# The experts' order in a mixture stage: two sparse experts behind each dense one

## The reference

```python
group_p = softmax(t @ w_group + b_group); g_w, g_idx = top_k(group_p, 1)
...
combine = g_w * one_hot(g_idx, N_GROUPS) * expert_w      # two experts of the token's group
for g in range(N_GROUPS):                                # 4 groups of 8 experts
    hg = silu(einsum('nd,edf->nef', t, w_gate[g])) * einsum('nd,edf->nef', t, w_up[g])
    y = y + einsum('nef,efd->nd', hg * combine[:, g, :, None], w_down[g])
```

## Time and profile before

| | us |
|---|---|
| median of 3 runs | 2664.12 |
| lowest and highest | 2663.37, 2664.22 |
| the profiled execution | 2666.28 |
| its span, first to last instruction | 2664.5 |

### The profile page before, as it was taken

The page is one execution under the profiler, slowest core; times in us unless marked ns, Lnnn a source line. Parts: engine busy times, 40 slices in busy tenths (PEclk is TensorE's granted clock), DMA queues, the critical chain, the costliest instruction groups (busy, mean ns, idle before and its releaser), DMA issues.

```text
span 2664.5 us, 45241 instructions
## 1 busy us (share of the span) xinstructions
PE 2621.3 (98%) x18380; PEld 2331.7 (88%) x18380; DVE 1802.6 (68%) x2201; ACT 1419.5 (53%) x1882; POOL 142.7 (5%) x229
## 2 busy tenths in 40 slices
PE   9999999999999999999989999999999999999999
PEld 8889989788898888879988888889988888889887
DVE  6667788766657666679757666666566676665765
ACT  6555567644555455458435455453355454455544
POOL 4000000100000000000210000000100000000000
PEclk9999999999999999999999999999999999999999
DMA  7187899655535555544305556556356555554553
GB/s 219 45 271 259 269 315 352 216 191 182 174 134 193 191 176 198 189 138 139 106 28 187 191 183 207 189 171 200 132 177 203 190 183 189 189 167 142 183 190 125
DMA packets 366195, 491.82 MB, mean 185 GB/s; under 512 B 12336, under 2 KB 321168, under 8 KB 366032
## 3 DMA queue, kind: packets, MB, share of 16 engines
q1 hardware_dynamic: 363008, 480.37, 54.6%
q0 software_dynamic: 2576, 7.97, 1.0%
q10 hardware_dynamic: 448, 1.12, 0.1%
HBM read 488.38 MB, written 1.05 MB: 184 GB/s over the span
## 4 chain that ended last, share of the span: by engine, by line
PE 91%; DVE 5%; ACT 3%; issue 1%; POOL 1%; DMA 0%; ACTq 0%; DVEq 0%; POOLq 0%
PE bank_all L368 22%; PE bank_all L367 11%; PE bank_all L347 8%; PE bank_all L349 8%; PE bank_all L348 8%; PE acc_all L347 8%; PE acc_all L349 8%; PE acc_all L348 8%; DVE w_lo L2062 1%; PE acc_all L3351 1%; PE bank_all L3359 1%; ACT w_hi L1947 1%; DVE w_lo L317 0%; PE bank_all L1846 0%; PE bank_all L1847 0%
## 5 line engine op out<-in xcount | busy, mean ns | idle before, releaser
L317 DVE TENSOR_TENSOR w_lo<-raw,w_hi 128x2048 fp32r<-128x2048 f32 x348 | 796.3, 2291 | 389.8 <-ACT w_hi L312 389.7
L312 ACT ACTIVATE w_hi<-raw 128x2048 fp32r<-128x2048 f32 x349 | 667.7, 1915 | 273.6 <-PE acc_all L349 222.4
L368 PE MATMUL bank_all<-act_both,w_hi 128*128 128x512 f32 x2560 | 654.8, 392 | 1.5 <-DVE w_lo L317 1.5
L368 PEld LDWEIGHTS bank_all<-act_both,w_hi 128*128 128x128 f32 x2560 | 465.2, 189 | 84.8 <-DVE w_lo L317 2.0
L367 PEld LDWEIGHTS bank_all<-act_both,w_lo 128*128 128x128 f32 x2560 | 349.2, 190 | 25.1
L347 PE MATMUL acc_all<-w_hi,mix_hi 128*128 128x512 f32 x920 | 360.9, 392 | 2.1 <-DVE mix_lo L3864 1.1
L349 PE MATMUL acc_all<-w_hi,mix_lo 128*128 128x512 f32 x920 | 358.6, 390 | 0.0
L348 PE MATMUL acc_all<-w_lo,mix_hi 128*128 128x512 f32 x920 | 358.1, 389 | 0.0
L367 PE MATMUL bank_all<-act_both,w_lo 128*128 128x256 f32 x2560 | 357.0, 282 | 0.0
L992 ACT ACTIVATE scratch<-bank_all 128x256 f32<-128x256 f32 x320 | 122.3, 385 | 426.1 <-PE bank_all L368 419.8
L347 PE MATMUL bank_all<-act_both,w_hi 128*128 128x256 f32 x1032 | 296.7, 288 | 7.4 <-DVE act_both L3678 2.6
(11 more groups left out here) (598 smaller groups left out, 3714.1 us busy)
## 6 DMA issues: line engine op xcount, KB each, us to landing
raw<-in_ffn_w_gu SPq DMA_DIRECT2D x176, 1024.0 KB, 5.1
raw<-in_ffn_w_down SPq DMA_DIRECT2D x88, 1024.0 KB, 4.9
raw<-in_ml_w_in SPq DMA_DIRECT2D x24, 1024.0 KB, 5.3
raw<-in_rt_w_in SPq DMA_DIRECT2D x24, 1024.0 KB, 5.1
raw<-in_w_up SPq DMA_DIRECT2D x20, 1024.0 KB, 7.5
raw<-in_w_down SPq DMA_DIRECT2D x19, 1024.0 KB, 6.3
raw<-in_w_gate SPq DMA_DIRECT2D x18, 1024.0 KB, 7.1
moe_raw<-in_w_gate SPq DMA_DIRECT2D x14, 1024.0 KB, 7.4
```

The source lines that it names most:

```text
L312: act.activation(w_hi[0:rows, slot, 0:size], raw[0:rows, slot, 0:size], ACT.Copy).then_inc(hi_made, 1)
L317: dve.tensor_tensor(w_lo[0:rows, slot, 0:size], raw[0:rows, slot, 0:size], w_hi[0:rows, slot, 0:size].bitcast(F32), ALU.subtract).then_inc ...
L368: return pe.matmul(bank[b][:, :], w_hi[:, slot, w], act_both[:, k, :], start=k == 0, stop=k == KT - 1)
```

## The change

The list of experts is made in another order. For e = 0 to 3 it is dense e, small 2e, small 2e+1; for e = 4 to 7 it is dense e, then two of the first middle group; the second middle group comes last, as before. The four gathers that are not made at the start move from steps 2, 4, 6 and 8 to steps 3, 6, 9 and 12, which are dense ones again. Panels, matmuls, DMAs and their sizes stay the same in number; their order on SP, ACT, DVE and PE follows the list. With a list of period three, D of expert i-3 now is of the same kind as expert i over the first 24 steps, but for steps 13 and 14; before, it was of the other kind in the mixed stretch.

```diff
--- before.py
+++ after.py
@@ -1673,7 +1673,11 @@
         moe_loaded = [sem(f"moe_loaded{i}") for i in range(RAW_RING)]
 
 
-        EXEC = [(r, e) for e in range(PER_GROUP) for r in (0, 3)] + [(r, e) for r in (1, 2) for e in range(PER_GROUP)]
+        EXEC = []
+        for e in range(PER_GROUP):
+            r = 3 if e < PER_GROUP // 2 else 1
+            EXEC += [(0, e)] + [(r, 2 * e % PER_GROUP + j) for j in range(2)]
+        EXEC += [(2, e) for e in range(PER_GROUP)]
         SPARSE = (3, 1, 2)
         HALF = P // 2
         MOE_PAN = {}
@@ -1686,7 +1690,7 @@
         MOE_ORDER = [("rows",), ("logits",), ("count",)] + [("gather", *g) for g in GATHERS[:2]]
         MOE_ORDER += [("back", 0), ("back", 1)] + [("share", j) for j in range(4)] + [("weight",)]
         MOE_SETUP = len(MOE_ORDER)
-        MOE_GATHER = {2 + 2 * j: g for j, g in enumerate(GATHERS[2:])}
+        MOE_GATHER = {3 + 3 * j: g for j, g in enumerate(GATHERS[2:])}
         MOE_USE, uses = {}, 0
         for i, (r, e) in enumerate(EXEC):
             MOE_ORDER += [("G", i)] + [("T", i - 1)] * (i > 0 and EXEC[i - 1][0] > 0)
```

## The result

| | before | changed |
|---|---|---|
| median of the runs on one chip (lowest to highest) | 2664.12 us (2662.95 to 2666.11, 5 runs) | 2676.59 us (2674.45 to 2680.07, 5 runs) |
| ratio, 95% interval | | 1.0047, [1.0037, 1.0058] |
| profiled execution, span | 2666.28, 2664.5 us | 2674.45, 2672.7 us |

The change costs 12.5 us. The forecast was 2677.3, range 2669 to 2686.

What follows compares the result with a forecast made beforehand. PE, busy 98% of the span, was taken as the bound, so only its idle time or clock could move. 14.4 + 2.1 - 3.3 = +13.2 us on the median 2664.12 gave 2677.3 us, range 2669 to 2686.

Steps and rivals of the forecast that it cites:

- Six short panels: Triples at steps 3, 6 and 9: PE waits 1.0, 1.9, 1.4 and 0.5 us behind each dense expert, +14.4 us.
- The first triple: Steps 0 to 2, no D yet: waits of 0.6, 2.0 and 2.2 us, 4.8 against 2.7 before, +2.1 us.
- The small group's end: Change-over to the middle group: its 2.5 us of waits and 0.8 us at the outputs go, -3.3 us.
- Dense with two middle experts: Steps 12 to 23: middle panels already hide their splits, taken as 0, with -0.8 us kept for the range.
- Loads: Moved loads on SP: cost 0, at most 1 us per triple, +4 us.
- one such fall: PE's clock, left out of the sum: one fall before, one kept; each in short panels costs 0 to 1.5 us.
- The clock in every triple: Rival: clock falls in every triple; three more falls give 2682 us, four at 3 us give 2688; chance 0.2.
- Short panels covered after all: Rival: splits get ahead, so the triples' waits vanish, 2660 to 2661 us; chance 0.1.
- interleaving regimes: Mixing dense and middle experts helps by itself, by the skill's rule; same number as the covered case, 2660 to 2661 us.
- Late loads: Rival: in the short stretch the pace of 2.9 us per load binds, up to 4 us more, 2681 us; chance 0.08.
- What it was to show: Profile signs: 19 us of waits for turn and `w_lo`, four groups between 160 and 285 us, middle experts at 8.6 us.

Runs made afterwards that it cites:

- Experiments 1: Kernel before with the new order for the small group only, middle experts left behind the last dense one: 2676.56 us, ratio 1.0049.
- experiment 6: Kernel before with all dense experts first, then eight small ones in a row, then the middle groups: 2688.72 us (one run).
- 2: Changed kernel with D of expert i-2 at step i instead of i-3: 2674.5 us, ratio 1.0038.
- 3: DVE makes a small expert's product before the split for D: changed kernel 2673.84 us, kernel before 2664.11 us.
- 4: ACT's copy and DVE's sum left out for small experts: changed kernel 2668.66 us, kernel before 2658.9 us (one run each).
- 5: DVE's split halved in columns for small experts' panels: changed kernel 2671.84 us, kernel before 2661.0 us (one run each).
- small_part: Kernel before with dense, small, small triples only, middle experts not mixed with dense ones: 2676.56 us, ratio 1.0049.
- first_old: Kernel before, with DVE making a small expert's product before the split for D: 2664.11 us, ratio 0.9996.

## Why the prediction was right

**Six short panels, +14.4.** Confirmed. Per triple the starts of PE's matmuls show, above their pace, 1.04 + 1.84 + 1.33 + 0.69 = 4.9 us (restarts included) at 196.3, 200.2, 203.7 and 206.3, and the fourth triple has 1.05 + 1.88 + 1.33 + 0.72 = 5.0; the prediction had 1.0 + 1.9 + 1.4 + 0.5 = 4.8. The third, with a clock fall, shows less idle time and takes 35.94 us, the fourth 35.95. So +14.7 to +15. Experiments 1 and 6 tie it to small experts in a row, 2 to the place of the long D, 3 and 4 to the product behind a split, 5 to the time that DVE takes for a split. It isn't the gather that each of the three triples holds: in experiment 6 the last gather stands ahead of the first small expert, and they wait all the same.

**The first triple, +2.1.** 0.78 + 2.48 + 1.69 = 4.95 us, against 0.79 + 2.15 = 2.94 before: +2.0. Its parts came out a little different (2.3 of idle time at the turn where 2.0 were forecast, 1.5 ahead of the dense G where 2.2 were): 166.1 is where the product starts on DVE, and the turn can start only when it is done, half a us later.

**The small group's end, -3.3.** Waits of 1.30 and 1.17 us and of 0.8 us are gone; with restarts 1.46 + 1.33 + 0.94 = 3.7. There is no wait of PE above 0.3 us between 278.3 and 449.2 in the changed kernel.

**Dense with two middle experts, 0.** Right within its bound of -0.8: 34.23 us for a dense and two middle ones.

**Loads, 0.** Right. None of PE's waits between 128 and 520 us is for a load, and no experiment showed one.

The waits come to 14.8 + 2.0 - 3.7 = +13.1, where the sum had +13.2. From the first dense G to the end of the stretch, the changed kernel takes 360.32 us (145.94 to 506.26) and the one before 349.47 (146.05 to 495.52): +10.85. Two things make up the difference. One is the clock: before, one fall lay in a long panel and cost 1.5 us; in the changed kernel the one fall of this stretch lay in a triple, where it cost nothing. The prediction said "before there is one such fall; I keep one", and at 170, where before had it, it wasn't kept. The other was put at nothing without being seen: the six waits of 0.2 us at the dense U of a pair, -1.2. With both the sum is +10.4. The 0.4 us that are left over are of the size of the small steps where one panel follows another (0.1 us in the first matmul behind a wait or a turn). small_part takes 360.21 us, so they are not the middle experts beside dense ones.

Outside that stretch the changed kernel lost 0.8 us ahead of it (the clock fell at 10 to 17 us), gained 0.9 in the setup (the first dense G comes 7.5 us after `first_gain`, before 8.4, with the clock at 0.65 from 141 to 144) and gained 2.55 between 1225 and 1386 us. Of these, 1.4 are a fall of the kernel before that the changed one didn't have, as its row shows (columns as in the earlier trace rows); the other 1.1 came between 1300 and 1371 us, with the clock at 1.00 in both, and are not explained.

```profile
1224.00:1227.40 3.40, 3.40 (x22) 3.40 (x23) 1.54 (x5) 1.04 (x3) 2.01 (x2) 0.67 0.61 214
```

Together that is the 8.2 us by which the profiled executions differ. The medians differ by 12.5, since the profiled one of the change was the fastest of its five runs (clock 0.998, the others 0.994 to 0.997) and that of before 2.2 us above its median. So the mechanism was right and its waits were sized to 0.1 us, but that the median was met to 0.7 us is in part luck: against the profiled execution the forecast was 2679.5, 5 us above the 2674.45 measured.

**The rivals.** The clock in every triple, 2682 to 2688: in small_part it fell in three of four, and that execution took 2676.0 us. The condition of this rival came about there, and its price was wrong, since the slow matmuls fill time in which PE would wait. The Trainium skill, in TensorE: Matmul & The Clock Gate, HAM oscillation, tells of a cost in every tile whose wait brings the clock down; here the falls came, and no cost of theirs could be seen. Short panels covered after all, 2660: the point it decides at, DVE being done with the product before PE ends the second small G (it is the product of the triple's first small expert, which the prediction calls the second), was missed by 1.7 us in three triples and by 2.3 in the first. By the Trainium skill's rule in Perfetto Trace Analysis, Optimization Strategy, interleaving regimes might have helped; the run with the dense and middle experts mixed and the one without do not differ (1.0047 and 1.0049), which agrees with the row that showed nothing to win. Late loads: no sign of them.

**What it was to show.** 19 us of waits: 17.2, or with restarts some 19.8. Those of the turn and of `w_lo` are 15.7 us against 4.8, 3.3 times as long and not four. Four groups between 160 and 285 us, none at the small group's end, middle experts at 8.65, the same busy time: all so.

No version that keeps all the work beats the kernel before. The nearest, first_old, is at 0.9996 [0.9987, 1.0006]. Not tried: a fourth slot of the ring, which would need room that I did not look for.

## What to carry to other kernels

An order that alternates long and short items works through the ring between producer and consumer: with three slots, the two items between must last as long as one production. So count, for a new order, how many short items follow each other (also those that run with a lag, as D here), and lay the producer's queue along them with the durations of one place in the old trace where this already happens. Such a place priced each triple here at 4.8 us, and it was 4.9 to 5.0. Look at the weight loads' waits too before calling PE busy throughout: 1.2 us were hidden there.

When waits are cut or added, price the clock by where its falls lie: in a stretch that the producer paces they cost nothing, over a long dense panel 1.5 us each (the dense G at 170.5; the dense D's of experiments 2 and 6: 1.4 to 1.6).

## What was not expected of the hardware

A fall of the clock within the waiting stretch was free to 0.02 us: the dense G starts at 206.33, 242.27 and 278.22 with granted clocks of 1.00, 0.59 and 1.00 just before, and at 206.32, 242.27 and 278.20 with 0.58, 1.00 and 0.62.

The same waits bring the clock down in one triple and not in the next. In the changed kernel triples 2 and 4 have the same waits to 0.06 us as triple 3 had up to its turn (0.89 and 1.73 us), and the clock fell in the third alone. In first_old it fell at the change-over, behind one wait of 1.7 us (0.77 from 336.6 to 340.0), where before, with waits of 1.3 and 1.2, it stayed at 1.00. So which wait brings it down could not be told from the wait's length here.
